# Row block 1 of the router: ScalarE's order, per-row scalars in VectorE's variance and Newton step, and three filler matmuls taken out

## What is computed

```python
for l in range(DEPTH):                                   # 2
    h = rms_norm(x, norm_mix_g[l])
    x = x + token_mixers(h, ...)                         # gMLP + sparse attention + gated conv, then @ w_out
    h = rms_norm(x, norm_ffn_g[l])
    x = x + hier_moe(h, ...)
return rms_norm(x, norm_final_g)

def rms_norm(x, g):
    return x * rsqrt(mean(x * x, axis=-1) + EPS) * g

def hier_moe(xt, ...):
    glog = xt @ rg_w + rg_b                              # 4 groups
    grp, gw = argmax(glog), softmax(glog)[argmax]
    elog = (xt @ re_w + re_b).reshape(-1, 4, 8)[grp]     # 8 experts in the chosen group
    tv, ti = top_k(elog, 2)
    tw = softmax(tv) * gw
    # each of the 32 experts takes the tokens that chose it:
    y = (silu(xb @ w_gate[e]) * (xb @ w_up[e])) @ w_down[e]
    out[token] += tw * y
```

## Time and profile before

| | us |
|---|---|
| median of 3 runs | 1388.49 |
| lowest and highest run | 1388.09, 1388.72 |
| the profiled execution's own time | 1389.1 |
| its span (first to last instruction) | 1386.2 |
| mean granted TensorE clock | 0.997 |
| PE busy | 1367.5 (99%) |
| DVE busy | 583.6 (42%) |
| ACT busy | 385.6 (28%) |
| POOL busy | 16.6 (1%) |
| DMA, all queues | 490.26 MB, mean 354 GB/s |

### The profile page before, as it was taken

The page is one execution under the profiler, slowest core; times in us unless marked ns, Lnnn a source line. Parts: engine busy times, 40 slices in busy tenths (PEclk is TensorE's granted clock), DMA queues, the critical chain, the costliest instruction groups (busy, mean ns, idle before and its releaser), DMA issues. The chain is left out here.

```text
span 1386.2 us, 18844 instructions
## 1 busy us (share of the span) xinstructions
PE 1367.5 (99%) x7808; PEld 803.4 (58%) x7808; DVE 583.6 (42%) x944; ACT 385.6 (28%) x707; POOL 16.6 (1%) x44
## 2 busy tenths in 40 slices
PE   9999999999999999999999999999999999999997
PEld 8899888544444444444488988884444444444442
DVE  7796646632222222222278956466222222222223
ACT  6455443211111111111164553441111111111112
POOL 0000000100000000000000000010000000000000
PEclk9999999999999999999999999999999999999999
DMA  9645668999999999999975557599999999999996
GB/s 309 224 166 185 245 227 311 417 406 423 429 426 429 428 426 427 426 427 420 406 233 190 213 184 271 183 377 399 418 426 428 428 426 428 427 427 428 423 422 257
DMA packets 89676, 490.26 MB, mean 354 GB/s; under 512 B 10686, under 2 KB 13816, under 8 KB 58872
## 3 DMA queue, kind: packets, MB, share of 16 engines
q1 hardware_dynamic: 89488, 489.03, 87.7%
q10 hardware_dynamic: 104, 0.03, 0.0%
HBM read 487.99 MB, written 1.05 MB: 353 GB/s over the span
## 5 line engine op out<-in xcount | busy, mean ns | idle before, releaser
L2151 PE MATMUL psB<-slots,uT 128*64 128x512 f32 x2016 | 455.7, 595 | 0.3 <-DVE uT L1572 0.2
L2151 PEld LDWEIGHTS psB<-slots,uT 128*64 128x64 f32 x2016 | 140.3, 137 | 263.8 <-issue 259.9
L2161 PE MATMUL psC<-slots,ybT_plain 128*64 128x512 f32 x1024 | 233.0, 598 | 1.7 <-DMA slots<-in_expert_w_down_dram 1.2
L1236 DVE TENSOR_TENSOR parts<-slots,parts 128x2048 fp32r<-128x2048 f32 (+1 forms) x80 | 177.6, 2248 | 69.9 <-ACT parts L1001 69.2
L1001 ACT ACTIVATE parts<-slots 128x2048 fp32r<-128x2048 f32 (+1 forms) x80 | 148.3, 1887 | 97.6 <-PE psB L1793 52.5
L1629 DVE TENSOR_TENSOR x<-x,psA 128x1024 f32<-128x1024 f32 x60 | 73.3, 1221 | 212.1 <-PE psA L2201 212.1
L1108 ACT ACTIVATE rel_parts<-psC 128x512 fp32r<-128x512 f32 x62 | 37.0, 597 | 385.6 <-PE psC L2161 210.6
L1793 PE MATMUL psB<-parts,hT_parts 128*128 128x512 f32 x448 | 139.0, 392 | 1.5 <-DVE parts L1236 1.0
L2161 PEld LDWEIGHTS psC<-slots,ybT_plain 128*64 128x64 f32 x1024 | 69.4, 136 | 117.0 <-issue 110.8
L1572 DVE TENSOR_TENSOR uT<-psA,g_ffn 128x512 f32<-128x512 f32 x64 | 44.3, 692 | 163.2 <-PE psA L2112 162.9
L1793 PE MATMUL psA<-parts,hT_parts 128*128 128x512 f32 x320 | 99.5, 392 | 0.0
(11 more groups left out here) (374 smaller groups left out, 1376.9 us busy)
## 6 DMA issues: line engine op xcount, KB each, us to landing
slots<-in_expert_w_down_dram SPq DMA_DIRECT2D x44, 2048.0 KB, 22.4
slots<-in_expert_w_gate_dram SPq DMA_DIRECT2D x40, 2048.0 KB, 22.7
slots<-in_expert_w_up_dram SPq DMA_DIRECT2D x40, 2048.0 KB, 21.5
slots<-in_w_in_dram SPq DMA_DIRECT2D x56, 1024.0 KB, 5.3
slots<-in_expert_w_gate_dram SPq DMA_DIRECT2D x44, 1024.0 KB, 10.6
slots<-in_expert_w_up_dram SPq DMA_DIRECT2D x42, 1024.0 KB, 10.9
slots<-in_expert_w_down_dram SPq DMA_DIRECT2D x28, 1024.0 KB, 11.1
slots<-in_expert_w_down_dram SPq DMA_DIRECT2D x24, 512.0 KB, 9.8
```

The source lines that it names most:

```text
L1236: v.tensor_tensor(low_part, mix_slot(i), high_part, ALU.subtract).then_inc(low_dve, 1)
L2151: ins = te.matmul(psB[j * BLK:(j + 1) * BLK, o, :], xT[:, 4 * half + c, j * BLK:(j + 1) * BLK], w, start=half == 0 and c == order[0], stop ...
L2161: ins = te.matmul(psC[j * BLK:(j + 1) * BLK, n, :], hidT[:, 2 * k + c, j * BLK:(j + 1) * BLK], w[:, c, n * 512:(n + 1) * 512], start=k == ...
```

## The change

Three edits. In ScalarE's program of the routing stage, `x_rounded(1, 1)` (round the upper half of x, row block 1) moves behind `upper_turned(1)` and `router_root(1)`. In `router_square` and `router_rstd`, which run for both row blocks of both layers, four two-tensor instructions on 128x1 become `tensor_scalar` with a per-row scalar as operand; the Newton step's sum is regrouped (the 1.5 is added in the second instruction). And `spin(3)` goes.

```diff
@@ router_norm, ScalarE @@
                     lower_turned(1)
                     left_rounded(1, 0)
                     act.wait_ge(dve_out, (l + 1) * len(on_dve))
-                    x_rounded(1, 1)
                     upper_turned(1)
                     router_root(1)
+                    x_rounded(1, 1)
                     left_rounded(1, 1)
                     sc.activation(spare[:, :], ones_plain[:, 0:1], ACT.Exp)
@@ router_square, router_rstd, VectorE @@
-                    link(v.scalar_tensor_tensor(var[:, t:t + 1], ss_upper[:, t:t + 1], 1.0 / D, ss[:, t:t + 1], ALU.mult, ALU.add))
+                    link(v.tensor_scalar(var[:, t:t + 1], ss_upper[:, t:t + 1], 1.0 / D, ss[:, t:t + 1], ALU.mult, ALU.add))
                     v.reciprocal(inv[:, t:t + 1], var[:, t:t + 1]).then_inc(inv_dve, 1)
...
-                    link(v.scalar_tensor_tensor(step, r, -0.5, r, ALU.mult, ALU.mult))
-                    link(v.tensor_tensor(step, step, var[:, t:t + 1], ALU.mult))
-                    v.scalar_tensor_tensor(r, step, 1.5, r, ALU.add, ALU.mult).then_inc(rstd_dve, 1)
+                    link(v.tensor_scalar(step, r, r, -0.5, ALU.mult, ALU.mult))
+                    link(v.tensor_scalar(step, step, var[:, t:t + 1], 1.5, ALU.mult, ALU.add))
+                    v.tensor_scalar(r, step, r, None, ALU.mult).then_inc(rstd_dve, 1)
                     dve.wait_ge(rstd_dve, l * 3 + t + 2)
@@ TensorE, before the ranking of row block 1 @@
                 for b in range(2):
                     gather_term(b, 2)
-                spin(3)
                 pe.wait_ge(members, l * 2 + 2)
                 ranked(psC[:, 0, 0:NE], order_b, 1, stop=True).then_inc(rank_ps, 1)
```

## The result

The changed kernel takes 1395.36 us (median, 1393.43 to 1397.98) against 1388.49 us (1387.56 to 1389.57): ratio 1.0050, 95% interval 1.0039 to 1.0061, 6.9 us slower. The forecast was 1388.4 us in a range to 1389.8, with 0.03 for slower by over 0.2%.

The account below looks back on a forecast made before the run. Transfers were taken to bound the expert stages, with TensorE having slack. TensorE gains 0.14 us in layer 0 and 0.66 in layer 1, 0.80 in all; 0.1 us let through gives 1388.4 us, range 1387.2 to 1389.8.

Parts of the forecast that it names:

- part 2: Variance and Newton step: four per-row forms cost 0 (bounds -0.1 and +0.1 us per layer); the order alone shortens L1289.
- The slack: Before each layer's last down projection: TensorE's idle 0.76 and 0.41 us, waiting for transfers, absorbs losses in routing.
- Part 1: ScalarE, row block 1: upper_turned going ahead of the rounding gains 0, at most 0.1 us.
- Part 2's other half: Variance in row block 1: new order takes 0.91 us off L1289 (1.07 to 0.16); L1305 comes 0.50 us earlier.
- Part 3: Choice (L1322), row block 1: held by GpSimd's later L873, so 0.14 of 0.50 us remains, bounds 0 and 0.50.
- rival (c): Choice not held: TensorE gains 0.50 us in layer 0, up to 1.0 in layer 1; same time; 0.72 with forecast and (d).
- Part 5: SP's queue: guest load issued about 0.3 us later, covered by transfers in flight; uncovered, 0.3 us per layer.
- Part 4: Three fillers removed before the ranking: 0 in layer 0, 0.66 us gained in layer 1, at most 1.0.
- (b): Without fillers TensorE idles and its clock drops: slower, 1389.9 us, or 1393.3 with two further uncovered stretches; chance 0.13.
- (d): GpSimd's subtraction still meets the variance; only the fillers' 0.5 us in layer 1 remain; 1388.4 us; 0.72 with forecast and (c).
- (a): TensorE's earlier arrival at the experts comes through whole: 1387.7 us, 1387.0 with upper bounds; chance 0.15.

Follow-up runs that it names:

- unlinked copy: Kernel before plus one VectorE copy of one number per row between router_rstd(0) and x_rest(1), without a semaphore: ratio 0.9997.
- ten more fillers: Kernel before with ten more filler matmuls behind the ranking of row block 1 (spin(11) for spin(1)): ratio 1.0038, 5.3 us slower.
- order and fillers: The change without its per-row scalars, so ScalarE's new order and spin(3) removed, against the kernel before: ratio 1.0005, median 1389.42 us.
- the linked copy: Kernel before plus one VectorE copy between router_rstd(0) and x_rest(1), which waits for its end; old forms, order and fillers kept: ratio 1.0049.
- the hole filled: Whole change plus five filler matmuls (spin(5)) in TensorE's hole before the transposes of row block 1: ratio 1.0010, 1.4 us slower than the kernel before.

## Why the prediction was wrong

**The step that failed** is in part 2: "a TENSOR_SCALAR on 128x2 takes 0.17 against 0.16, so I take 0 for all of them, bounds -0.1 and +0.1 us per layer". The per-row form takes 0.21, so four of them cost 0.2 us in each row block, twice the bound already. In row block 0, 0.17 us of it reach L1278. The size alone was not the fault: in row block 1 they cost nothing that could be measured. The fault was to cost them at nothing without naming what is late next in row block 0. There VectorE goes straight on to L1278, and GpSimd is 0.06 us behind. The sign of it stood in the earlier trace rows: L878 at 1.67 us, where its like took 1.15. I took that row for a length of GpSimd's and worked out everything from it for row block 1, but did not ask who had held it in row block 0, and by how little. The Trainium skill's rule that I had cited (SBUF — State Buffer, Who interferes with whom) names both sides of it: whoever issues first has the shared ports for the whole instruction, and a VectorE instruction with at most one SBUF input, outside the two-port modes, keeps out of it. These runs agree with both, the first with 1.61 us at L1278, the second with 0.21 us beside GpSimd; in which mode the new forms ran, no run shows. Close to a tie the starts in a profile don't decide: with the unlinked copy L1278 started 0.01 us second and still went first. I used the rule only on the edit's own row block.

**The slack.** "What it loses is free up to the slack" was wrong as well. The idle times at the earlier trace rows were read as TensorE's reserve against transfers that run on their own. They don't at the start: SP issues the guest load behind `rstd_dve`, and the next six loads behind the first expert matmuls (258.27 us before, 260.52 after), and the DMA engines had thin stretches there even before, 352 GB/s at 277 us. When the stage starts late, they get thinner (381 instead of 417 GB/s from 249 to 277 us), and the last transfer lands late by as much. A wait for a transfer stands at 29 of the 32 last down projections (in one of them it falls inside), between 0.36 and 1.77 us and without regard to the delay, so the landing moves with the start. That the thin stretch is the way by which it goes through I infer from the issue times. The run with ten more fillers agrees, 384 GB/s with the guest load on time, but no run held those loads back alone.

**What was right**, in layer 0 of the run with order and fillers. Part 1: upper_turned gained nothing (the route starts 8.20 us behind L1538 instead of 8.15, so it lost 0.05). Part 2's other half: L1289 at 0.16 us from the order alone, and L1305 earlier by 0.37 us where 0.50 was forecast: the route was those 0.05 us later, and L1305 started 0.13 us behind its end, not 0.05. Part 3: the choice held by L873 and ending 0.14 us earlier (12.04 against 12.18 us behind L1538), as forecast, so rival (c) fell. Part 5: the guest load 0.30 us later, where 0.3 was forecast. Part 4 is seen in layer 1 of the run without the fillers: the ranking starts 0.52 us earlier against L1538, the 0.66 without part 3's 0.14. In the changed kernel the race had moved everything.

**The rivals.** (b) had the right sign and part of the mechanism: the clock did fall, in layer 0 too, and cost 3.1 us of the 5.9 by which the first expert matmuls of the change stand behind those of order and fillers. But its cause was not the place of the fillers: taken out alone they changed nothing, and the linked copy lost 6.8 us with all of them in place. It was TensorE's new idle time of 1.50 us ahead of the transposes, since with that time filled the clock stayed at 2.4 GHz. A slack that isn't there made its price too small, and 0.03 for slower by over 0.2% followed from both errors. (d) fell: L1289 stood for 0.16 us. (a) stays open. With order and fillers the first expert matmuls came 0.15 and 0.83 us earlier, and the time did not fall (1.0005, 0.9996 to 1.0014); but with no slack in front a gain should come through, and no run had one large enough to tell.

From the parts to the whole, by the starts in one profile each: 2.84 us for the race and 3.09 for the clock, both layers, make 5.9 us against the order-and-fillers kernel. That one took 1389.42 us in its runs, and 1395.3 is within the scatter of the changed kernel's 1395.36. The sum holds, the split is rough: by the ratios to the kernel before (1.0005, with the hole filled 1.0010, the change 1.0050) it would be 0.7 us for the race by itself and 5.5 for the clock. In either reckoning the clock has half of the loss or more.

## What to carry to other kernels

Where two engines hold each other's instructions, read the long one of each pair: a length of 1.67 instead of 1.15 us says that it lost, and the distance of the two starts says by how little. Before adding even 0.2 us in front of the winner, ask what happens when it loses, and if there is a hole elsewhere, take the instruction out of the race. A wait at the end of a stage is no reserve until some run has started that stage late and found it shorter.

## What was not expected

- The point is sharp: L1278 starting 0.07 us later costs nothing, in the change it starts 0.17 us later and the kernel loses 6.9 us. Even 0.01 us behind GpSimd it still went through.
- The per-row tensor_scalar on 128x1 takes 0.21 to 0.22 us, the two-tensor form 0.16, in every row block and kernel.
- The low clock comes and goes with hardly a difference on TensorE: the kernel before with L1278 moved ahead, profiled twice, had 3.4 us of it in layer 1 the first time and in layer 0 the second. There it set the first expert matmul of the one layer 0.95 and 0.67 us behind that of the other.
